# Expert input rows fetched by indirect transfer, and half of a side stream of sums moved, in a two-block transformer kernel

## The reference

```python
# first block, expert layer (h: the normed, modulated rows, 256 x 1024)
logits = h @ w_router + b_router
top_val, top_idx = lax.top_k(logits, 4);  gates = softmax(top_val)
# rows of h are sorted by expert, and for every expert e:
gu  = xe @ w_gate_up[e] + b_gate_up[e]                # 1024 -> 2048
g   = minimum(gu[:, :1024], 7);  u = clip(gu[:, 1024:], -7, 7)
act = (u + 1) * (g * sigmoid(1.702 * g))
y   = act @ w_down[e] + b_down[e]                     # summed back with the gates
# second block, each layer l
mod = silu(c) @ ada_w[l] + ada_b[l]                   # 6 x 1024: shifts, scales, gates
modc = silu(c_ctx) @ ada_w[l] + ada_b[l]
h = modulate(rms_norm(x, mix_pre_g[l]), sh1, sc1);  p = h @ w_in[l]
y = (ga * attn @ w_attn_o + gg * gmlp @ w_gmlp_o + gc * conv31(p) @ w_conv_o) @ w_out
x = x + g1 * rms_norm(y, ...);  h2 = modulate(rms_norm(x), sh2, sc2);  x = x + g2 * rms_norm(mlp(h2))
```

## Time and profile before

| what | us |
|---|---|
| median of 3 runs | 3129.35 |
| profiled execution, whole | 3139.97 |
| its span | 3138.2 |
| TensorE busy in the span | 2965.7 (95%) |
| VectorE busy | 1325.8 (42%) |
| ScalarE, GpSimd busy | 476.8, 55.5 |
| expert layer (282.39 to 1585.02) | 1302.63 |

### The profile page before, as it was taken

One profiled execution on the slowest core, in us unless ns is written; L12 is line 12 of the kernel. 1 busy time (PEld: TensorE's weight loads), 2 busy tenths in 40 slices (PEclk: granted clock), 3 DMA queues, 4 the chain that ended last, 5 costly groups with the idle time before them and its releaser, 6 DMA issues.

```text
span 3138.2 us, 30984 instructions
## 1 busy us (share of the span) xinstructions
PE 2965.7 (95%) x12068; PEld 1742.1 (56%) x12068; DVE 1325.8 (42%) x3177; ACT 476.8 (15%) x948; POOL 55.5 (2%) x85
## 2 busy tenths in 40 slices
PE   5997999999999999999889999999999999999998
PEld 3464345444555444544367768644444577587764
DVE  6755423566652121111326953273773258731201
ACT  1212001122212110010112031100000111311100
POOL 0000000000000000000000000000000000000000
PEclk9977999999999999999999999999999999999999
DMA  8554999999998988999943413343432244124342
GB/s 338 205 221 186 394 374 395 374 370 392 396 381 357 388 331 359 372 389 399 395 196 141 160 54 134 134 161 115 180 136 79 97 145 148 67 108 146 123 161 94
DMA packets 107297, 752.89 MB, mean 240 GB/s; under 512 B 12368, under 2 KB 12752, under 8 KB 18544
## 3 DMA queue, kind: packets, MB, share of 16 engines
q1 hardware_dynamic: 93888, 691.05, 55.8%
q0 software_dynamic: 6912, 46.14, 3.8%
q10 hardware_dynamic: 6352, 13.71, 1.2%
HBM read 741.68 MB, written 9.18 MB: 239 GB/s over the span
## 4 chain that ended last, share of the span: by engine, by line
PE 84%; DMA 9%; DVE 4%; ACT 1%; issue 1%; DVEq 0%; SPq 0%; ACTq 0%
PE ps L525 26%; PE ps L537 17%; PE ps L832 9%; DMA ring<-stream 9%; PE ps L747 8%; PE ps L913 7%; PE ps L743 3%; PE ps L1111 2%; PE ps L557 2%; PE ps L1099 1%; PE ps L839 1%; PE ps L586 1%; PE ps L1045 1%; PE ps L1025 1%; PE ps L847 1%
## 5 line engine op out<-in xcount | busy, mean ns | idle before, releaser
L525 PE MATMUL ps<-area,ring 128*128 128x256 f32 (+1 forms) x3328 | 822.1, 409 | 0.3
L525 PEld LDWEIGHTS ps<-area,ring 128*128 128x128 f32 x3328 | 634.8, 191 | 184.5 <-issue 108.1
L537 PE MATMUL ps<-ring,area 128*128 128x512 f32 x1216 | 528.4, 596 | 3.2 <-DVE area L2125 3.2
L832 PE MATMUL ps<-ring,area 128*64 128x512 f32 x2112 | 477.9, 598 | 36.4 <-DMA ring<-stream 35.4
L537 PEld LDWEIGHTS ps<-ring,area 128*128 128x128 f32 x1216 | 231.9, 191 | 290.2 <-issue 285.1
L832 PEld LDWEIGHTS ps<-ring,area 128*64 128x64 f32 x2112 | 146.6, 137 | 349.6 <-issue 265.4
L747 PE MATMUL ps<-area,ring 128*128 128x256 f32 x1152 | 254.7, 379 | 0.1
L913 PE MATMUL ps<-ring,area 128*64 128x512 f32 x1056 | 239.4, 606 | 6.9 <-ACT area L2357 5.2
L747 PEld LDWEIGHTS ps<-area,ring 128*128 128x128 f32 x1152 | 216.1, 190 | 28.2 <-issue 0.3
L1894 DVE SCALAR_TENSOR_TENSOR area<-area,cols 128x256 f32<-128x256 f32 x480 | 202.6, 485 | 1.1
L913 PEld LDWEIGHTS ps<-ring,area 128*64 128x64 f32 x1056 | 74.0, 139 | 152.3 <-issue 142.1
(11 more groups left out here) (344 smaller groups left out, 2153.4 us busy)
## 6 DMA issues: line engine op xcount, KB each, us to landing
ring<-stream SPq DMA_DIRECT2D x634, 1024.0 KB, 8.8
area<-shared_modulation POOLq DMA_DIRECT2D x40, 1024.0 KB, 6.9
area<-modulation SPq DMA_DIRECT2D x16, 1536.0 KB, 6.4
expert_rows<-area ACTq DMA_DIRECT2D x62, 128.0 KB, 7.4
x<-x_tiles ACTq DMA_DIRECT2D x1, 1024.0 KB, 12.5
area<-ctx_tiles ACTq DMA_DIRECT2D x1, 1024.0 KB, 4.8
out<-x SPq DMA_DIRECT2D x2, 512.0 KB, 2.6
cst<-constants ACTq DMA_DIRECT2D x1, 929.5 KB, 13.9
```

Source lines behind the costliest of these rows:

```text
L525: i = mm(ps[:, b, 0:n], w[:, k % 4, j * P:(j + 1) * P], rhs(k), start=(k == 0), stop=(k == 4 * kgs - 1))
L537: i = mm(ps[:, b, :], lhs(k, t), w[:, k % 4, :], start=(k == 0), stop=(k == 4 * kgs - 1))
L832: i = mm(ps[half(h), bank, :], xT[:, k % 4, half(k // 4)], w[:, 2 * (k % 2) + h, :], start=(k == 0), stop=False)
```

## The change

- **Rows by transfer.** ACT stores the 256 input rows to a DRAM table `rows_h` (four transfers of 256 KB, before the expert layer). From block 2 on no `gather` runs: in block e TensorE multiplies `sel` of block e + 2 with a table of token numbers, one column wide (`find_rows`, 4 products), behind the up product; DVE copies the 128 row numbers out (`slot_at`) behind the hidden rows; GpSimd fetches 128 pieces of 2 KB (256 KB) by one indirect transfer into one of two buffers `xes`; `turn_rows` of block e + 1 waits for it. The rows of blocks 0 and 1 still come by `gather`, and ACT's copy L2336 stays for these alone.
- **Bias.** `bgu` is [4 x 32 partitions, 512] in place of [32, 2048]; the four bias products of a block use 32 rows each and stand together ahead of the gate product (`biases`), waiting for `pickrow`, which DVE now picks one block ahead.
- **Bank.** The down product of blocks 0 to 30 goes to bank 7 (`APART`), not to bank 1 beside the up product.
- **Sums.** Chunks 8 to 15 are summed in blocks 6 to 13 (`SUMFROM`, `LATE`; loads in blocks 6 to 12). Chunks 16 to 23 are summed in layer 0 of the second block (`middle_sums`: 8 x 18 steps, 12 of them behind each of the 8 `cg` pairs, the rest ahead of the convolution steps in `fill`), from two buffers loaded by GpSimd. `coefficients` is done in two parts.
- **Fill.** The attention loops of both layers use `fill(3)` in place of `fill(1)`.

```diff
+LATE = 16
+SUMFROM = 6
-MOD_AT = [None] * FIRST + [at for e in range(NBLK) for at in mods_in(e)][:MODS - FIRST]
+MOD_AT = [None] * FIRST + [at for e in range(SUMFROM, NBLK) for at in mods_in(e)][:LATE - FIRST] + [None] * (MODS - LATE)
...
+            def biases(tag, before):
+                pe.wait_ge(*before("row"))
+                for n in range(4):
+                    r = slice(NE * n, NE * n + NE)
+                    i = mm(ps[half(n % 2), (GATE, UP)[n // 2], :], pickrow[r, :], bgu[r, :], start=True, stop=False)
+                i.then_inc(*mark("biases_added", (tag, "bias")))
...
+            def find_rows(n):
+                pe.wait_ge(*at(("sel", n)))
+                if n > 2:
+                    pe.wait_ge(*at(("found", n - 1)))
+                for h in range(2):
+                    for t in range(TT):
+                        i = mm(ps[half(h), XROW, 0:1], sel[:, t, :], stat("token", 4)[:, 2 * h + t:2 * h + t + 1], start=(t == 0), stop=(t == TT - 1))
+                i.then_inc(*mark("places_full", ("places", n)))
...
+                if main and e + 2 < NBLK:        # DVE, behind the hidden rows
+                    n = e + 2
+                    dve.wait_ge(*at(("places", n)))
+                    if n >= 4:
+                        dve.wait_ge(inputs_came[n % 2], 16 * (n // 2 - 1))
+                    V.tensor_copy(slot_at[:, n % 2:n % 2 + 1], ps[:, 2, 0:1]).then_inc(*mark("rows_found", ("found", n)))
...
+            pool.wait_ge(inputs_stored, 64)
+            for e in range(NBLK):
+                m = FIRST + e - SUMFROM
+                if FIRST <= m < LATE:
+                    pool.wait_ge(*at(("part2", m)))
+                if FIRST <= m and m + 1 < LATE:
+                    pool.dma_start(mods2, mods2_d[m + 1]).then_inc(shared_landed, 16)
+                n = e + 2
+                if n < NBLK:
+                    pool.wait_ge(*at(("found", n)))
+                    pool.wait_ge(*at((("moe", n - 3) if n > 2 else ("first", "moe"), "xTr")))
+                    nc.gpsimd.indirect_dma_start(xes[n % 2], None, rows_h, bass.IndirectOffsetOnAxis(ap=slot_at[:, n % 2:n % 2 + 1], axis=0)).then_inc(inputs_came[n % 2], 16)
...
+                def middle_sums():
+                    for m in range(LATE, MODS):
+                        dve.wait_ge(later_landed[m % 2], 16 * (1 + (m - LATE) // 2))
+                        yield from modulation_steps(m, modsm[m % 2], part2l, part2lt)
...
                     TT_(glp[:, k, 0:ns, PADT:PADT + SEQ], segs(ps[:, B(ka), 0:N]), segs(tmp[:, k % 4, 0:N]), ALU.mult).then_inc(*mark("products_taken", ("drained", ka)))
+                    for _ in range(12):
+                        next(middle, 0)
...
                     for _ in range(n):
-                        if next(taps, 0) == 0:
+                        if next(middle, 0) == 0 and next(taps, 0) == 0:
                             return
...
-                    fill(1)
+                    fill(3)
```

More of the change, by code:

```diff
@@ L832, in project @@
                         i = mm(ps[half(h), bank, :], xT[:, k % 4, half(k // 4)], w[:, 2 * (k % 2) + h, :],
-                               start=(k == 0), stop=False)
+                               start=False, stop=(k == KD - 1))
                     if k % 2:
[L835 to L841, removed]
+                        i.then_inc(*mark("weights_used", (tag, "chunk", first + k // 2), *([(tag, name)] if k == KD - 1 else [])))
+            def biases(tag, before):
[4 more added lines that the diff above has]
+                i.then_inc(*mark("biases_added", (tag, "bias")))
             def gather(tag):
@@ L875, in expert @@
                 project(tag, e, "up", UP, 4)
+                if sums and e + 2 < NBLK:
+                    if e == 0:
+                        pe.wait_ge(*at((tag, "xe")))
+                    find_rows(e + 2)
                 if scattered:
@@ L879, in expert @@
                 if upcoming:
-                    turn_rows(tag)
+                    turn_rows(tag, e + 1 if sums else 0)
                 else:
@@ L889, in expert @@
                 if weighed:
+                    if sums and e + 2 >= NBLK:
+                        pe.wait_ge(*at(("found", NBLK - 1)))
                     pe.wait_ge(*at((tag, "selg")))
@@ L1747, in expert @@
                     summed(tag, 0)
+                if main and e == 0:
+                    dve.wait_ge(*at((tag, "rows")))
+                    choose_ahead(2)
                 dve.wait_ge(*at((tag, "up")))
@@ L1789, in _ @@
             choose(first, 0)
-            V.memset(selgT, 0.0).then_inc(*mark("vector_steps", ("zero", "moe")))
+            for n in range(4):
+                TS(stat("token", 4)[:, n:n + 1], con("lane", 1), float(P * n), None, ALU.add).then_inc(*mark("vector_steps"))
             busiest_then(first)
             iotae_b = con("iotae", NE).unsqueeze(1).unsqueeze(1).to_broadcast([P, TT, TOPK, NE])
+            V.tensor_copy(pickrow, onehot[:, 0:1].to_broadcast([P, CAP])).then_inc(*mark("row_picked", (first, "row")))
             places()
@@ L1819, in _ @@
                     choose(("first", tag), 0)
+                    dve.wait_ge(*at((("moe", NBLK - 1), "bias")) if p == 1 else last("row_picked"))
+                    V.tensor_copy(pickrow, onehot[:, 0:1].to_broadcast([P, CAP])).then_inc(*mark("row_picked", (("first", tag), "row")))
                     dve.wait_ge(*at((("first", tag), "rows")))
```

141 lines of the change are left out of this document (90 added, 51 removed).

## The result

| | before | changed |
|---|---|---|
| median, us (4 runs each) | 3131.89 | 3106.44 |
| range, us | 3128.22 to 3134.81 | 3104.90 to 3108.81 |
| ratio, 95% interval | | 0.9917 (0.9901 to 0.9933) |
| profiled execution, its span, us | 3139.97 | 3104.90, 3103.1 |

Faster by 25 us, and shown to be so: the interval ends at 0.9933. A second measurement of the changed kernel (e10) gave 0.9908 (0.9895 to 0.9921).

What follows compares the result with a forecast made beforehand. TensorE, busy 95% of the span, was taken to bound the kernel, with some expert blocks bound by DMA bytes or a mixed floor. Terms -31 + 16 - 4 = -19 took 3139.97 to 3121, less 10.6 a median of 3111; range 3094 to 3130.

Steps and rivals of the forecast that it cites:

- the likeliest case: Whole kernel: the forecast itself, median 3111 us, own range 3100 to 3122, chance 0.61.
- the floor: Expert-layer blocks with two held pieces: DMA stream, then TensorE's work after the last up chunk, sets about 39.5 us.
- Expert layer, -31: Expert layer: block-by-block sum of less TensorE work, fewer loads and added fetches, -31 us, bounds -16 and -50.
- the rest: Remaining expert-layer blocks: 18 and 28 +0.4 each, the others -0.3 or nothing, together -1.7 us.
- A alone: Expert-layer blocks 18 and 28, with one of two held pieces, bound by bytes: +0.4 us each.
- The standstill: Block 22: DMA engines stand still some 3 us while a held piece is worked on; was to absorb the fetch.
- rival 2: Expert layer: the stream pays for fetches in all blocks, bias quarters run one after the other; 3126 us, chance 0.10.
- Layer 0, +16: Layer 0, second block: 144 sum steps on DVE displace convolution steps to the layer's end; +16 us.
- Layer 1, -3.8: Layer 1: 16 more steps in attention remove the end wait of 4.73; -4.7 + 0.9 = -3.8 us.
- Rival 1: Expert layer: blocks with both held pieces follow TensorE's work, a further dozen gain 1.7 us; 3091 us, chance 0.10.
- Rival 3: Expert layer from block 2: fetch comes late, TensorE stands at turn_rows; 3142 us at 38 us delay, chance 0.07.
- Rival 4: Layer 0: sums run DVE out of cover already in cg; layer costs 30, not 16; 3125 us, chance 0.12.

Runs made afterwards that it cites:

- e10: The changed kernel measured again without an edit, beside the kernel before: 3106.91 us, ratio 0.9908 to the kernel before.
- e2: Changed kernel with the selecting products multiplied again in blocks 1 to 30, result unused, fetches kept: 3119.84 us, ratio 0.9945 to the kernel before.
- e3: Changed kernel with each of the 31 fetches issued twice, the second into spare buffers: 3113.64 us, ratio 0.9920 to the kernel before.
- e5: Changed kernel with fill(1) again in place of fill(3) in both layers' attention loops: 3122.18 us, ratio 0.9951 to the kernel before.
- e6: Changed kernel with 46 convolution steps put into DVE's idle time before layer 0's attention outputs: 3093.59 us, ratio 0.9857 to the kernel before.
- e11: The same edit of the changed kernel as e6, run again in more rounds: 3087.71 us, ratio 0.9858 to the kernel before.
- e9: Changed kernel with selecting products back in all blocks and find_rows, row-number copy and fetches removed: 3117.07 us, ratio 0.9942 to the kernel before.
- e4: Changed kernel with modulation chunks 16 to 23 summed in the expert layer again, none in layer 0: 3105.0 us, ratio 0.9894 to the kernel before.

## Why the prediction was right

Forecast -18 from the median shown (the sum was -19, and 3110.4 was put down as 3111), measured -25; 3106.4 lies in the range of the likeliest case. Its mechanism held in the parts that were run apart: the floor (e2), the fetch that the stream does not pay in full (e3), the convolution steps at the end of the layers (e5, e6, e11). The miss of 7 us is a matter of sizes.

**Expert layer, -31 against -37.** By groups of blocks, on the means named above (the length of one block mostly scatters by up to about 2 us between traces of the same code, that of block 9 by 2.5, of block 32 by 3.3 and of block 11 by 5):

| blocks | forecast | traced |
|---|---|---|
| 0, 1 | -3 | -2.9 |
| 2 to 5 | -12.5 | -10.5 |
| 6 to 9 | -1.2 | -2.7 |
| 10 to 12 | +0.1 | -1.4 |
| 13, 14 | -3.2 | -3.5 |
| 15 to 17 | -6.2 | -5.4 |
| 20 | -2 | -2.9 |
| 24 | -1 | -1.9 |
| the rest | -1.7 | -6.3 |

- *The floor* held in size: blocks 19, 22, 27, 29 and 30 take 39.5 us each in the mean (197.5 in all; 198.0 before), the value used, though single ones lie between 38.7 and 40.0 in the first trace. e2 shows that TensorE's work ahead of the last up chunk does not set it.
- *Blocks 2 to 5*: 3 to 5 fell to it or below (38.83, 38.80, 39.54 in the first trace), but block 2 stayed at 42.34 with TensorE idle for 3.9 us. It follows two blocks bound by bytes, and starts with nothing in reserve. That explanation is only argued.
- *The rest* is the term that was mis-sized most, and most of it is in blocks with one piece: 18, 21 and 28 together fell by 3.3 us (1.3, 1.9 and 0.1), where the fetch was to make 18 and 28, which have A alone, longer by 0.4 each; block 23 fell by 1.6. e3 has the three at 98.3 us with twice the fetches, e9 at 99.2 with none, changed at 98.6: so the bytes of the fetch do not show in them, within a scatter of 1.8 us between the two traces of before. What shortened them stays open.
- *TensorE's terms*: gather 1.72 gone; bias 0.90 gone (forecast 0.9), the quarters do run side by side; `find_rows` 0.33 (forecast 0.6). Together 2.3 a block where 2.0 was forecast; block 16 shows 2.19. The Trainium skill ("TensorEngine Tiling (Array Packing)", Key Properties) has a change of tiling mode drain TensorE; 1.02 us for eight records between ordinary products leaves room for 0.06 above the 0.96 of one pair, so at this size the rule is not seen.
- *The fetch*: 0.26 MB each. The standstill is shallower with it (0.32 in place of 0.00 at one place in block 22), as the forecast had it. e3 puts 31 further ones at 1 to 4 us, and at 8 at most, where rival 2 asked for 19.5.

**What each part brought.** In the expert layer: moving eight sums out of it 22 us (e4), product to fetch 10 (e2, e9). Some 5 of the 37 are left for the bias quarters, the bank and the shift of the first loads. None of these three was run alone, and 5 us is no more than such a difference is uncertain by. Over the whole kernel the sums come back in layer 0 (21 us), so the gain is 10 of the fetch, 5 of the rest, 1 of the sums and 12 of `fill(3)` in the two layers (e5), which the prediction had counted but not set apart. That makes 28 where the stages show 26, as near as these parts can be measured. The moved sums, one of the two changes that the title names, brought nothing that can be seen.

**Layer 0, +16 against +16.0.** The wait at the sum over features was to grow from 4.73 by 13.7 to 18.4 and is 17.40. The sums in `gelu` cost 0.5 instead of 2.2: two waits for a bank of 0.20 and 0.31. The attention adds waits of 1.10 and 0.41, where 0.9 was forecast. These make 14.7 of the 16.0; what the other 1.3 are was not followed. The `gelu` with its bank waits, and the larger wait of the attention:

```profile
1637.77 3.72 PE L533 MATMUL ps<-area,ring 128*128 128x256 f32 x16 [0.20 <-DVE area L2003]
1641.80 27.73 PE L545 MATMUL ps<-ring,area 128*128 128x512 f32 x64 [0.31 <-DVE area L2003]
1786.46 1.37 PE L565 MATMUL ps<-cst,area 128*128 128x128 f32 x8 [1.10 <-DVE area L2109]
```

That the two numbers agree so closely is in part luck. The forecast's +16 held -0.8 for the start, which lies outside the 16.0, and 2.2 for `gelu` where 0.5 came; against that stand the larger waits of the attention and the 1.3 that nobody followed.

**Layer 1, -3.8 against -4.8.** No wait at the sum over features is left, as forecast. e5 confirms the reason: without the 16 steps of `fill(3)` the layer takes 6.3 more, where 16 x 0.43 - 0.9 = 6.0.

**The rivals.** Rival 1 (no floor) falls by e2: by it, e2 would have cost 52 us. Rival 2 falls by e3 and by the 1.02 us of the biases. Rival 3 (fetch late) falls: it lands 7.3 us after its issue (median) where 37 are to be had, and nothing waits at `turn_rows`. The page that it cites from the Trainium skill ("SBUF — State Buffer", SBUF: two separate sides) warns of DVE holding up GpSimd's descriptor writes. The prediction took the issues of the earlier trace rows to have run beside DVE's work and to speak against such a stall. They do not: DVE was idle during seven of those eight. It was idle during 25 of the 31 issues of the changed kernel too, since DVE's copy of the row numbers releases the fetch, and in most blocks DVE then waits some 6 us for its next operation, as in block 3:

```profile
403.12 0.15 DVE L1822 CAST slot_at<-ps 128x1 uint32<-128x1 f32 x1
403.55 0.95 POOL L2645 DMA_INDIRECT area<-input_rows,slot_at  x1 [37.87 <-DVE slot_at L1822]
409.33 0.42 DVE L1619 TENSOR_TENSOR area<-ps,cst 128x256 f32<-128x256 f32 x1 [6.05 <-ACT cst L2347]
```

The 31 issues took 947 to 1024 ns. So no stall came, but the warning was hardly put to the test; rival 3 falls by the landing times and by the missing wait. Rival 4 (cover lost in `cg`) falls by layer 0 itself.

**The offset.** 10.6 us were taken off for the profiled execution, which was a long one: in its repetition (3129.45) the expert layer alone is 6.6 us shorter. An offset of that kind does not enter a difference, so the step was sound.

## What to carry to other kernels

Ask of each stage what it has to spare before pricing an edit: 52 us of TensorE's work were worth 10, and 8 MB of transfers, 19.5 us at the full rate, 8 at most. Each mostly fell into time in which the other was waited for. Work that is moved to make room must be followed to the place where it now ends: the sums moved for 22 us cost 21 there, until the steps they displaced were put into idle time that already stood in the profile. That idle time was named in the prediction and cost 16 to 19 us to leave empty.

## What the runs showed of the hardware

- Products one column wide are cheap: eight records of `find_rows` took 0.33 us, 41 ns each (128 x 64 weights). The 32 columns of the earlier trace rows took 120 ns each, with weights of 128 x 128; how much of the difference comes from the columns and how much from the weights no run shows.
- Four products on quarters of the rows took 1.02 us for 128 x 512 outputs in all, as one pair on the full rows does.
- An indirect transfer of 128 pieces of 2 KB lands in 6.8 to 8.4 us beside the ring's stream (median 12.5 for the 512 KB ones in the changed kernel). 31 further ones added 8 us at most to the kernel.
- Two executions of one kernel differed by 6.6 us in the expert layer, 0.5% of it, and five with the same code there by 10.1. The first pair of traces alone would have given -43 instead of -37.
